# The beginning of a two-block kernel in another order: x before the memory tokens

## The reference, cut to what matters

```python
mem_n = rms_norm(mem, mem_norm)
for i in range(DEPTH):                                   # DEPTH = 2
    hn = rms_norm(h, norm_pre[i])
    mkv = (mem_n @ w_mem_kv[i]).reshape(B, M, 2, MEM_HEADS, MEM_DIM)
    k_m, v_m = mkv[:, :, 0], mkv[:, :, 1]
    if i % 2 == 0:
        proj = hn @ w_in_a[j]
        c_q, c_kv, k_r, q_m, gate = split_cols(proj, [Q_LORA, KV_LORA, MLA_ROPE, MEM_WIDTH, MIX_WIDTH])
        main = mla_mixer(c_q, c_kv, k_r, positions, ...)
...
    mem_out = memory_attention(q_m, k_m, v_m)
...
x = second_block(first_block(x, mem, ...), c_2, ...)
```

## Time and profile before

| what | value |
|---|---|
| median of 3 executions (lowest, highest) | 1906.64 us (1902.64, 1910.74) |
| the profiled execution's own time | 1904.96 us |
| its span, first to last instruction | 1903.0 us |
| PE busy | 1862.1 us (98%) |
| DVE, POOL, ACT busy | 1094.0, 789.8, 758.9 us |
| mean granted TensorE clock | 0.997 |

### The profile page before, as it was taken

One profiled execution on the slowest core, in us unless ns is written; L12 is line 12 of the kernel. 1 busy time (PEld: TensorE's weight loads), 2 busy tenths in 40 slices (PEclk: granted clock), 3 DMA queues, 4 the chain that ended last, 5 costly groups with the idle time before them and its releaser, 6 DMA issues.

```text
span 1903.0 us, 23803 instructions
## 1 busy us (share of the span) xinstructions
PE 1862.1 (98%) x9841; PEld 1485.9 (78%) x9841; DVE 1094.0 (57%) x1597; ACT 758.9 (40%) x1181; POOL 789.8 (42%) x361
## 2 busy tenths in 40 slices
PE   7999999999999999999999999999999999999998
PEld 5788666977666798977788888887977878888886
DVE  5325766658767669445588647865931465512543
ACT  5436754431564421374333123324475343312332
POOL 2234743434663552123344444443444434444432
PEclk9999999999999999999999999999999999999999
DMA  7225013554204342122243444453441223233221
GB/s 256 77 61 137 23 42 105 178 178 155 89 23 133 111 155 67 45 89 88 82 160 124 156 143 134 152 164 98 136 144 45 84 72 107 70 111 111 81 77 65
DMA packets 212060, 205.96 MB, mean 108 GB/s; under 512 B 21351, under 2 KB 209003, under 8 KB 211952
## 3 DMA queue, kind: packets, MB, share of 16 engines
q1 hardware_dynamic: 209369, 200.36, 33.2%
q0 software_dynamic: 1472, 3.72, 0.7%
q10 hardware_dynamic: 1111, 0.36, 0.1%
HBM read 201.44 MB, written 2.11 MB: 107 GB/s over the span
## 4 chain that ended last, share of the span: by engine, by line
PE 91%; ACT 3%; DVE 3%; POOL 2%; DMA 1%; issue 1%; ACTq 1%; SPq 0%; DVEq 0%
PE bank L552 59%; PE bank L1178 17%; PE bank L812 2%; PE bank L862 2%; PE bank L834 2%; PE bank L989 2%; POOL wl L2539 1%; PE bank L1253 1%; PE bank L492 1%; PE bank L575 1%; PE bank L817 1%; ACT probs L1577 1%; ACT wh L1407 1%; PE bank L1240 1%; DMA ring<-in_w_mem_kv 0%
## 5 line engine op out<-in xcount | busy, mean ns | idle before, releaser
L2539 POOL TENSOR_TENSOR wl<-ring,wh 128x2048 fp32r<-128x2048 f32 (+4 forms) x145 | 614.9, 4241 | 874.2 <-ACT wh L1407 871.9
L1407 ACT ACTIVATE wh<-ring 128x2048 fp32r<-128x2048 f32 (+5 forms) x147 | 254.8, 1733 | 314.3 <-PE bank L1178 126.3
L552 PE MATMUL bank<-xfh,wh 128*128 128x512 f32 x704 | 275.4, 391 | 0.4 <-DVE xfl L1999 0.2
L552 PE MATMUL bank<-xfl,wh 128*128 128x512 f32 x704 | 274.1, 389 | 0.0
L552 PE MATMUL bank<-xfh,wl 128*128 128x512 f32 x704 | 274.0, 389 | 0.0
L1929 DVE SCALAR_TENSOR_TENSOR acc<-ring,cs,acc 128x256 f32<-128x256 f32 x336 | 235.0, 699 | 12.0
L552 PEld LDWEIGHTS bank<-xfh,wh 128*128 128x128 f32 x704 | 132.1, 188 | 31.8 <-DVE xfl L1999 2.5
L552 PEld LDWEIGHTS bank<-xfh,wl 128*128 128x128 f32 x704 | 132.1, 188 | 27.7
L552 PEld LDWEIGHTS bank<-xfl,wh 128*128 128x128 f32 x704 | 132.2, 188 | 26.9
L2397 DVE SCALAR_TENSOR_TENSOR x<-bank,mod,x 128x512 f32<-128x512 f32 x48 | 34.7, 751 | 179.0 <-PE bank L1178 179.0
L1178 PE MATMUL bank<-hsph,wh 128*128 128x512 f32 x352 | 137.5, 391 | 0.0
(11 more groups left out here) (426 smaller groups left out, 3998.0 us busy)
## 6 DMA issues: line engine op xcount, KB each, us to landing
ring<-in_ada_w SPq DMA_DIRECT2D x48, 1024.0 KB, 5.1
ring<-in_ffn_w_in SPq DMA_DIRECT2D x44, 1024.0 KB, 5.1
ring<-in_w_in_b SPq DMA_DIRECT2D x14, 1024.0 KB, 5.3
ring<-in_even_w_in SPq DMA_DIRECT2D x14, 1024.0 KB, 5.2
ring<-in_ffn_w_out SPq DMA_DIRECT2D x16, 768.0 KB, 4.4
ring<-in_odd_w_in SPq DMA_DIRECT2D x12, 1024.0 KB, 5.5
ring<-in_ffn_w_out SPq DMA_DIRECT2D x16, 640.0 KB, 4.1
ring<-in_w_out SPq DMA_DIRECT2D x8, 1024.0 KB, 5.2
```

The source lines that it names most:

```text
L552: mm = eng.matmul(o, l_, r_, start=(first and i == 0), stop=(last and i == 2))
L1407: eng.activation(wh[:, m % SPLIT, h:w], ring[:, n % RING, h:w], ACT.Copy).then_inc(wh_ready, 1)
L2539: eng.tensor_tensor(wl[:, m % SPLIT, h:w], ring[:, n % RING, h:w], wh[:, m % SPLIT, h:w].bitcast(F32), ALU.subtract).then_inc(wl_ready, 1)
```

## The change

x is loaded first, in two halves of 512 columns with a semaphore each, and turned and normed first. The memory is loaded behind the first two weight chunks, turned behind the first projected chunk and normed while the chunks behind it run. The memory's values and keys of each layer become four ordinary chunks between `in_a.kr` and `in_a.qm`, split by ACT and POOL like all others: values with 256 moving columns (`tokens`), keys already turned, with 256 moving columns (`features` with n=M), so the turning of the keys goes. The scaled x tiles go through two PSUM banks, `mod_bank` and `ssq_bank`, and no longer through `tmp_a`. The squares of the memory, its root, and the sine and cosine of the positions move to other places in the lists of ACT and DVE. Behind `in_a.qm` the lists are as before. The core of the diff:

```diff
@@ -135,13 +135,12 @@
             for _ in range(behind[n] if n < len(behind) else 0):
                 plan.append(ada.pop(0))
 
-    for l in range(DEPTH):
-        add(k8("mem.v", a["w_mem_kv"][l], M, 2 * M))
-    for l in reversed(range(DEPTH)):
-        add(k8("mem.k", a["w_mem_kv"][l], 0, M))
     w = a["w_in_a"][0]
-    add(k8("in_a.cq", w, 0, 256) + k8("in_a.cq", w, 256, 512) + k8("in_a.kr", w, 512, 672)
-        + k8("in_a.qm", w, 672, 928))
+    add(k8("in_a.cq", w, 0, 256) + k8("in_a.cq", w, 256, 512) + k8("in_a.kr", w, 512, 672))
+    for name, lo in (("mem.v", M), ("mem.k", 0)):
+        for l in range(DEPTH):
+            add(k8(name, a["w_mem_kv"][l], lo, lo + M))
+    add(k8("in_a.qm", w, 672, 928))
     add(k8("in_a.gate", w, 928, 1952))
     q = a["w_q_up_a"][0].rearrange("(t p) (h n) -> p t h n", p=P, n=NOPE + ROPE)
     add([("q_rope", q[:, :, :, NOPE:], 3, HEADS * ROPE), ("q_nope", q[:, :, 0:6, 0:NOPE], 3, 6 * NOPE),
@@ -318,13 +317,11 @@
...
-        x_tok, m_tok, vec_tok = at("x_tok", 32, NB, D), at("m_tok", 48, 2, D), at("vec_tok", 56, VEC_TILES, P)
-        mem_n = at("mem_n", 64, KT, M)
-        mh, ml = pair("mem", 80, 88, KT, M)
+        x_tok, m_tok, vec_tok = at("x_tok", 32, NB, D), at("m_tok", 88, 2, D), at("vec_tok", 56, VEC_TILES, P)
+        mem_n = at("mem_n", 80, KT, M)
+        mh, ml = pair("mem", 64, 72, KT, M)
-        tmp_a = at("tmp_a", 106, 2, S)
...
@@ -679,79 +657,74 @@
                     b = bank(("vec", n), "dve")
                     done(eng.transpose(b[:, 0:rows], vec_tok[0:rows, n, :], ident[0:rows, 0:rows]))
...
+            def turn_memory():
+                pe.wait_ge(loaded_m, 16)
+                for k in range(0, KT, 2):
+                    b = bank(("mT", k), "dve")
+                    for j in range(4):
+                        t = eng.transpose(b[:, j * P:(j + 1) * P],
+                                          m_tok[:, j % 2, (k + j // 2) * P:(k + j // 2 + 1) * P], ident)
+                    done(t)
+            def sum_memory():
+                pe.wait_ge(ssq_taken, counts["hn"])
+                for k in range(4):
+                    i = counts["sq"]
+                    pe.wait_ge(sq_ready, i + 1)
+                    group_sums(sq[:, i % 2, 0:M], range(2), k == 0, False)
+                    group_sums(sq[:, i % 2, M:2 * M], range(2), False, k == 3).then_inc(sq_used, 1)
+                    counts["sq"] += 1
+                counts["hn"] += 1
             for k in range(KT):
...
+                pe.wait_ge(loaded_x[k // 4], 16)
                 b = bank(("xT", k), "dve")
                 for j in range(NB):
                     t = eng.transpose(b[:, j * P:(j + 1) * P], x_tok[:, j, k * P:(k + 1) * P], ident)
                 done(t)
+                if k == 3:
+                    turn_vectors()
                 if k >= 2:
                     ssq(k - 2, KT)
             for k in range(KT - 2, KT):
                 ssq(k, KT)
...
+            warm(2, n=S // 2)
+            norm_spread((scaled, KT))
+            warm(3, n=S // 2)
+            m, ws = chunk("in_a.cq")
+            wide([("cq", t) for t in range(2)], "act", ws, xa, KT, "x_a")
+            chunk_done(m)
+            turn_memory()
+            m, ws = chunk("in_a.cq")
+            features(("cq", 2), "act", ws, slice(0, P), xa, KT, "x_a")
+            sum_memory()
+            features(("cq", 3), "act", ws, slice(P, 2 * P), xa, KT, "x_a")
+            chunk_done(m)
             m, ws = chunk("in_a.kr")
             features(("cq", 4), "act", ws, slice(0, P), xa, KT, "x_a")
...
+            norm_spread((mem_normed, KT), 2)
             features(("kr",), "act", ws, slice(P - NOPE, P + ROPE), xa, KT, "x_a")
             chunk_done(m)
...
+            for l in range(DEPTH):
+                m, ws = chunk("mem.v")
+                for b in range(2):
+                    tokens(("vm", l, b), "act", ws, slice(0, M), (mh, ml), KT, b, "mem")
+                chunk_done(m)
+                for t in ((0, 1), (2,))[l]:
+                    ssq(t, 3)
+            for l in range(DEPTH):
+                m, ws = chunk("mem.k")
+                for t in range(2):
+                    features(("km", l, t), "act", ws, slice(t * P, (t + 1) * P), (mh, ml), KT, "mem", n=M)
+                chunk_done(m)
+                if l == 0:
+                    for t in range(2):
+                        ssq(t, 2)
             m, ws = chunk("in_a.qm")
             features(("in_a.qm", 0), "act", ws, slice(0, P), xa, KT, "x_a")
...
             norm_spread((cq_normed, 3))
             features(("in_a.qm", 1), "act", ws, slice(P, 2 * P), xa, KT, "x_a")
             chunk_done(m)
@@ -1321,6 +1294,10 @@
                     done(t)
             assert len(chunks) == len(plan)
+        def xa_tmp(t):
+            return (mod_bank, ssq_bank)[t % 2][:, :]
         def odd_y_of(h):
             return og[:, h, :] if h < 2 else tiles[index[("yb", h)]][3][:, :]
@@ -1360,14 +1337,16 @@
         def _(eng):
             sp = Engine(eng)
             eng.dma_start(consts[:, :], a["const_f32"][:, 0:C_COLS]).then_inc(loaded_c, 16)
-            eng.dma_start(m_tok[:], a["mem"][0].rearrange("(b p) d -> p b d", p=P)).then_inc(loaded_m, 16)
+            for half in range(2):
+                cols = slice(half * S, (half + 1) * S)
+                eng.dma_start(x_tok[:, :, cols], a["x"][0][:, cols].rearrange("(b p) d -> p b d", p=P)).then_inc(loaded_x[half], 16)
             load_vectors(eng, 2)
             for n, (name, src, kt, cols) in enumerate(plan):
-                if n == DEPTH:
-                    eng.dma_start(x_tok[:], a["x"][0].rearrange("(b p) d -> p b d", p=P)).then_inc(loaded_x, 16)
+                if n == 2:
+                    eng.dma_start(m_tok[:], a["mem"][0].rearrange("(b p) d -> p b d", p=P)).then_inc(loaded_m, 16)
                 if n >= RING:
                     user = chunks[n - RING]
-                    sp.wait_ge({"pe": wl_ready, "ada": ada_done, "mem": mem_low}[user], chunks[:n - RING + 1].count(user))
+                    sp.wait_ge({"pe": wl_ready, "ada": ada_done}[user], chunks[:n - RING + 1].count(user))
                 dst = ring[:, n % RING, 0:kt * cols].rearrange("p (t n) -> p t n", t=kt)
                 if len(src.shape) == 4:
                     for t in range(kt):
@@ -1400,7 +1379,8 @@
                 while used["w"] < min(upto, len(released)):
                     m = used["w"]
                     n = pe_at[m]
-                    act.wait_ge(*(released[m - SPLIT] if m >= SPLIT else (filled, mark["mem.v"])))
+                    if m >= SPLIT:
+                        act.wait_ge(*released[m - SPLIT])
                     act.wait_ge(landed[n % RING], landing[n])
                     w = plan[n][2] * plan[n][3]
                     h = w // 2 if m in halved else 0
@@ -1466,44 +1446,22 @@
             act.wait_ge(loaded_c, 16)
             load_roots()
...
             def square_memory(k):
                 wait_emptied(act, ("mT", 2 * k))
                 square(mem_n[:, 2 * k:2 * k + 2, :])
...
             for k in range(KT):
                 wait_emptied(act, ("xT", k))
                 square(x[:, k, :])
                 if k == 3:
                     split_weights(1)
...
             root()
...
+            for t in range(KT):
+                used["n"] += 1
+                high(xa_tmp(t), xa[0][:, t, :], scaled, used["n"])
+                if t == 1:
+                    split_weights(2)
             def square_lora(t):
@@ -1514,21 +1472,32 @@
                 dst = cq[:, t, :] if t < 3 else ckv[:, t - 3, :]
                 empty(("cq", t), dst)
                 if t == 1:
...
+                    for k in range(4):
+                        square_memory(k)
+                if t == 2:
+                    root(2 * GROUP)
+                if t == 3:
                     act.wait_ge(angle_ready, 1)
                     eng.activation(sin[:, :], sin[:, :], ACT.Sin).then_inc(sin_ready, 1)
                     eng.activation(cos[:, :], cos[:, :], ACT.Sin).then_inc(sin_ready, 1)
                     load_roots()
...
+            for t in range(KT):
+                high(mem_n[:, t, :], mh[:, t, :], mem_normed, t + 1)
+            for t in range(2):
                 square_lora(t)
             empty(("kr",), kr[ropes, :], part=(ropes, slice(0, S)))
...
+            half_bank = (slice(0, P), slice(0, M))
+            for l in range(DEPTH):
+                for b in range(2):
+                    empty(("vm", l, b), vm[:, l, b, :], part=half_bank)
+                for t in ((2,), (3, 4))[l]:
+                    square_lora(t)
+            for l in range(DEPTH):
+                for t in range(2):
+                    empty(("km", l, t), km[:, l, t, :], part=half_bank)
+                if l == 0:
+                    root()
             split_weights(tile_chunk[index[("in_a.qm", 0)]] + 2)
...
             root()
             for t in range(2):
```

(22 more changed lines are left out.)

132 lines of the change are left out of this document (7 added, 125 removed).

## The result

The changed kernel takes **1917.1 us** (median of 6 executions, 1912.85 to 1917.69) against 1905.92 of the kernel before in 6 (1902.64 to 1910.74): ratio **1.0046, 95% interval 1.0026 to 1.0066**. The profiled execution took 1917.48 us, its span is 1915.4 (before 1903.0), its mean granted clock 0.993 (before 0.997).

What follows compares the result with a forecast made beforehand. The prediction took PE's chain of waits as the bound and priced the change as the first gate matmul's time: 107.6 + 1.2 - 103.5 = +5.3 us, from 1904.96 to 1910.3, set at 1911 towards the median; range 1903 to 1918.

Steps and rivals of the forecast that it cites:

- forecast of no difference above 0.5%: Whole kernel: time within about 9.5 us of the kernel before, chance 0.85; slower 0.12, faster 0.03.
- the clock staying down over two memory chunks: Memory chunks: granted clock near 1.2 GHz for two of four, +14 to +15 us, 1920; whole slower-clock rival has chance 0.09.
- First projected product at 24.0: Start: first chunk's load lands at 14.5, then ACT's conversion, squares and root; PE starts projecting at 24.0.
- First chunk, 11.2 us, PSUM for nothing: First projected chunk: PE runs from 24.0 to 35.2; x tiles lying in PSUM priced at nothing.
- Second and third chunk, 26.5 us: Memory turning, both chunks, memory sums, spreading and `kr`: PE is through at 61.7, from 35.2.
- POOL holds the memory's low part: Ahead of memory chunks: low parts start at 61.3, not 57.7, behind POOL's subtraction; PE waits 5.3 us, starting at 67.0.
- The first rival: Memory's first low part begins before POOL's subtraction, saving 3.6 us; with an earlier load 1905.5 to 1908; chance 0.25.
- Four memory chunks, 27.4 us: Memory chunks, 67.0 to 94.4: 5.9 us each, plus sums and waits of 1.0 at the second, 1.3 at the fourth.
- both slower rivals: Clock stays down in memory chunks, 1920 or 1931, chance 0.09; 96 additional weight loads unhidden, 18 us, 1929, chance 0.01.
- To the gates, 13.2 us: From memory chunks to first gate matmul: 13.75 as before, without 0.57 of sums, reaching 107.6.
- The clock, 1.2 us: PE idling before the first chunk and the memory chunks may each lower the clock, 0 to 1.5; 1.2 for both.
- whatever that gains or loses, the end gains or loses: Behind the first gate matmul all lists are as before, so its shift alone was priced as the whole change.

Runs made afterwards that it cites:

- memory in PSUM: Changed kernel with the scaled memory tiles written to two PSUM banks instead of SBUF; median 1907.8 us, ratio 0.9999 to the kernel before.
- warm attention: Changed kernel with seven warming calls instead of one in PE's wait for the second attention's first probabilities; median 1912.1 us, ratio 1.0026 to the kernel before.
- warm gap: Changed kernel with three warming calls in PE's wait ahead of the first memory matmul; median 1908.1 us, ratio 1.0007 to the kernel before.
- x in SBUF: Changed kernel with the scaled x tiles back in two SBUF tiles instead of PSUM banks; median 1915.6 us, ratio 1.0065 to the kernel before.
- start too: Changed kernel: scaled memory in PSUM, three attention warming calls, two ahead of x, parameter vectors turned later, two ACT conversions moved; 1902.5 us, ratio 0.9984 to before.

## Why the prediction was right, and where it was not

The forecast of no difference above 0.5% and the range 1903 to 1918 held; the centre was 6.1 us low. That the range held is in part luck: the median stands 0.9 us below its upper end, that end came from the clock staying down over two memory chunks, which did not happen, and what filled the gap was a fall at 500 us that the prediction did not have. By its steps:

1. *First projected product at 24.0*: it came at 25.68. The load was sized well (14.5; ACT began at 14.87, and where it had nothing else to do it saw the load at 15.06). Mis-sized was what follows: from ACT's conversion to the root's end 5.9 us passed instead of 4.9, as PE turned x at half pace until 19.05, with 1.05 us for four transposes instead of 0.59. The step took 4.9 from a place where the clock was at full for all but the last sums. The other runs with the same order to this point bear this out: where the clock's first record stands at 11.31 ("memory in PSUM") it took 4.6 and the product came at 24.32, where it stands at 16.69 ("warm attention", seven calls) 5.0 and 24.69, and where the clock fell again at 17.72 ("warm gap") the product came at 26.63.
2. *First chunk, 11.2 us, PSUM for nothing*: 11.42, and the low parts of x kept 0.68 to 0.69 us beside POOL. Right; "x in SBUF" shows what was avoided.
3. *Second and third chunk, 26.5 us*: 27.1 (37.10 to 64.2). Right.
4. *POOL holds the memory's low part*: 4.16 us, ending with POOL; PE waited 4.9 (5.3 predicted). Right, in cause and size. The first rival, that the hold does not occur, fell.
5. *Four memory chunks, 27.4 us*: 28.8. The first took 8.00 us instead of 5.9 at the low clock; the waits for POOL were 0.81 at the third, 0.27 at the fourth and 0.23 at `in_a.qm`, instead of 1.0 at the second and 1.3 at the fourth. The weight loads of the 256-column products stayed hidden, and the clock was back at 73.7, so both slower rivals fell.
6. *To the gates, 13.2 us*: 13.1.
7. *The clock, 1.2 us*: **this is the term that was mis-sized.** Ahead of the gates the clock cost some 2.4 us, 1.0 at the start (step 1) and 1.4 at the memory chunks ("warm gap"), which is about half of the step from 5.3 to 7.5; the other half is spread over steps 1 to 3. Behind the gates the prediction said that "whatever that gains or loses, the end gains or loses", and priced nothing; there the clock gave back 3.4 us at half pace at 430 and took 17.1 us at half pace at 500.

Without its clock term the prediction's sum is +4.1 us; at full clock the runs show +5.6, with the slow start still in it. The mechanism of the loss ahead of the gates was right; that nothing arises behind them was not. What was missing is that a single execution of the kernel before stands anywhere in a spread of 14 us, by falls of the clock at places far from the change.

## What to carry to other kernels

Where a kernel's time spreads, look at the granted clock of every run before explaining a difference of a few us: fit time against clock, compare at one clock (and see in the pace of the first instructions whether the start was slow, which the mean clock does not hold), and fill the short waits of PE at which the clock falls. A wait that an engine's hold causes is mended by room in front of it as well as by taking the hold away (2.9 and 3.0 us at full clock). And behind an edit that takes one wait away, read the lists of the other engines again: here POOL's pace, then ACT's sines, took its place, and only the third edit in a row paid.

## What the runs showed of the hardware

- Two waits of PE of 1.41 and 0.70 us, 0.5 us of work between them, were enough for a fall of the clock of 17.1 us in one execution and for none in another. That the falls there end when the first is filled and the second is cut to 0.58 us is shown (10 of 10 executions at 0.996 or above); why one execution falls and another does not was not tried.
- With the same instructions up to that point, the clock's first record, at full, stands at 19.05 us in the changed kernel's trace and at 10.9 in that of "warm gap"; four transposes took 1.05 us until 18.5 in the one and 0.59 from 13.6 on in the other. The windows print 1.00 ahead of that record, and the mean clock does not count the slow start.
- A call of two 512-column float32 matmuls on the identity takes 1.02 us at full clock, and two such calls ahead of x took 3.78, before the clock's first record at 8.24 ("start too"): warming work has to be sized like any other.
